# Identity matmuls in eight places ahead of TensorE's stages

## What is computed

```python
def first_block(x, ...):
    n1 = rmsnorm(h, norm1_g[l])
    proj = n1 @ w_in[l]                       # GLA and SGU branches, gates
    merged = sigmoid(ga) * (y_a @ w_branch_a) + sigmoid(gb) * (y_b @ w_branch_b)
    h = h + merged @ w_out[l]
    n2 = rmsnorm(h, norm2_g[l])
    h = h + peer(n2, ...)                     # 8 heads, top 16 of 128 x 128 experts each
    return rmsnorm(h, final_g)

def hybrid_layer(x, ...):
    x = x + 0.5 * rms_norm(swiglu(rms_norm(x, ffn1_pre_g), ...), ffn1_post_g)
    h = rms_norm(x, mix_pre_g)
    proj = h @ w_in                           # attention and SSM branches
    mixed = concatenate([attn, ssm]) @ w_out
    x = x + rms_norm(mixed, mix_post_g)
    x = x + 0.5 * rms_norm(swiglu(rms_norm(x, ffn2_pre_g), ...), ffn2_post_g)
    return x
```

## Time and profile before

| what | value |
|---|---|
| median of three runs | 1694.07 us |
| the profiled execution | 1692.44 us |
| its span, first to last instruction | 1690.7 us |
| PE busy | 1582.9 us (94%) |
| DVE busy | 1235.1 us (73%) |
| ACT busy | 795.9 us (47%) |
| POOL busy | 155.4 us (9%) |
| mean granted TensorE clock | 0.971 |
| matmul instructions in the records | 9080 |

### The profile page before, as it was taken

How to read it: one execution, slowest core, us unless ns; L and a number is a source line. 1 busy time by engine, 2 the same in 40 slices (tenths; PEclk the granted TensorE clock), 3 DMA queues, 4 the chain that set the end, 5 groups by cost and what they waited for, 6 DMA issues and landing times.

```text
span 1690.7 us, 25985 instructions
## 1 busy us (share of the span) xinstructions
PE 1582.9 (94%) x9080; PEld 1363.3 (81%) x9080; DVE 1235.1 (73%) x2038; ACT 795.9 (47%) x1212; POOL 155.4 (9%) x85
## 2 busy tenths in 40 slices
PE   6989889989999999999999999799997988879997
PEld 5777778879998888878888888688877967568886
DVE  4575559999998777677777777677777685367776
ACT  4544345447776343344444444544445653254443
POOL 1000257860000000000000000000001200000000
PEclk9999999999999999999999999899997989889999
DMA  5444334532324555555555555355552322345552
GB/s 199 175 147 171 131 125 163 187 125 100 115 108 151 197 198 189 183 174 199 180 192 191 183 196 198 137 191 189 183 194 78 139 75 100 125 139 196 185 187 99
DMA packets 38952, 270.40 MB, mean 160 GB/s; under 512 B 4705, under 2 KB 5217, under 8 KB 6642
## 3 DMA queue, kind: packets, MB, share of 16 engines
q1 hardware_dynamic: 37296, 266.97, 44.2%
q10 hardware_dynamic: 1602, 2.71, 0.5%
HBM read 268.62 MB, written 1.05 MB: 160 GB/s over the span
## 4 chain that ended last, share of the span: by engine, by line
PE 80%; DVE 15%; ACT 3%; issue 1%; DMA 1%; DVEq 0%; SPq 0%; ACTq 0%
PE ps L696 47%; PE ps L731 17%; PE ps L733 7%; PE ps L943 3%; DVE arena L1857 2%; PE ps L685 1%; DVE wlo L525 1%; PE ps L730 1%; DVE arena L1835 1%; PE ps L802 1%; DVE arena L1815 1%; DVE arena L1818 1%; DVE arena L1824 1%; DVE arena L1812 1%; DVE arena L1821 1%
## 5 line engine op out<-in xcount | busy, mean ns | idle before, releaser
L731 PE MATMUL ps<-XT,whi 128*128 128x512 f32 x1200 | 430.9, 399 | 1.9 <-DVE wlo L525 1.9
L696 PE MATMUL ps<-XT,whi 128*128 128x256 f32 x1696 | 315.6, 305 | 4.2 <-DVE wlo L525 4.2
L733 PE MATMUL ps<-XT,wlo 128*128 128x256 f32 x1050 | 295.6, 281 | 0.0
L504 ACT ACTIVATE whi<-raw 128x1024 fp32r<-128x1024 f32 x178 | 187.3, 1058 | 221.6 <-PE ps L696 161.2
L525 DVE TENSOR_TENSOR wlo<-raw,whi 128x1024 fp32r<-128x1024 f32 x146 | 186.5, 1289 | 121.5 <-ACT whi L504 120.2
L696 PE MATMUL ps<-whi,HAh 128*128 128x512 f32 x688 | 269.7, 392 | 5.5 <-DVE HAl L1943 3.0
L696 PEld LDWEIGHTS ps<-XT,whi 128*128 128x128 f32 x1696 | 268.0, 196 | 4.6 <-issue 4.6
L696 PE MATMUL ps<-wlo,HAh 128*128 128x512 f32 x688 | 268.8, 391 | 0.0
L696 PE MATMUL ps<-whi,HAl 128*128 128x512 f32 x688 | 268.3, 390 | 0.0
L731 PEld LDWEIGHTS ps<-XT,whi 128*128 128x128 f32 x1200 | 223.8, 189 | 47.4 <-DVE wlo L525 2.2
L733 PEld LDWEIGHTS ps<-XT,wlo 128*128 128x128 f32 x1050 | 199.6, 190 | 5.9
(11 more groups left out here) (267 smaller groups left out, 2104.1 us busy)
## 6 DMA issues: line engine op xcount, KB each, us to landing
raw<-in_experts SPq DMA_DIRECT2D x128, 1024.0 KB, 4.7
raw<-in_panels SPq DMA_DIRECT2D x58, 1024.0 KB, 4.8
raw<-in_ffa SPq DMA_DIRECT2D x33, 1024.0 KB, 4.8
raw<-in_ffb SPq DMA_DIRECT2D x33, 1024.0 KB, 4.8
arena<-in_row_post ACTq DMA_DIRECT2D x3, 512.0 KB, 3.7
X<-in_x SPq DMA_DIRECT2D x2, 512.0 KB, 5.3
out<-X SPq DMA_DIRECT2D x2, 512.0 KB, 2.7
arena<-in_row_ln ACTq DMA_DIRECT2D x2, 256.0 KB, 7.5
```

Of the source, the lines that this page charges most:

```text
L504: act.activation(whi[:, buf(p), :], half(item_of(p), p % 2), ACT.Copy).then_inc(part_hi, 1)
L696: last = pe.matmul(out, x if w_moving else w, w if w_moving else x, start=start and n == 0, stop=stop and n == 2)
L731: last = pe.matmul(out, wh[:, k], XT[:, k], start=k == 0, stop=k == NK - 1)
L733: pe.matmul(out[:, T:], wl[:, k], XTh[:, k], start=False, stop=False)
```

## The change

PE gets a helper `keep_turning`, which multiplies `ident` by `ident` n times into 128 columns of a bank, and `turn_ahead`, which first claims the second bank of the coming stage's transposes. It is called ahead of seven `transposes` calls, with n of 18, 30, 50, 62, 52, 36 and 50, and `keep_turning` alone with 20 ahead of the first `output`. That makes 318 matmuls. No other engine's list changes.

```diff
+            def keep_turning(out, n):
+
+                for _ in range(n):
+                    pe.matmul(out[:, 0:P], ident[:, :], ident[:, :], start=True, stop=True)
+
+            def turn_ahead(stage, n):
+
+                t_claim(pe, stage, 1)
+                keep_turning(t_bank(stage, 1), n)
...
+            turn_ahead("mg", 18)
             transposes("mg", tiles(XN, NK), waits=lambda j: (merged, 2 + j // 2 * 2))
...
+            turn_ahead("n2", 30)
             transposes("n2", tiles(XN, NK), norm=1)
...
+            turn_ahead("idx", 50)
             pe.wait_ge(sel_ready, 1)
             transposes("idx", [s[:, tt, :] for s in (I1S, I2S, GS) for tt in range(NT)])
...
             for i in range(4):
                 claim(pe, f"ex{i}")
+            keep_turning(bank("ex3"), 20)
             for n in range(UN):
                 output(n, S_PRE + n, S_PRE + n + 1, n % 2, start=(n == 0))
...
+            turn_ahead("ffa", 62)
             transposes("ffa", tiles(XN2, NK), norm=2)
...
+            turn_ahead("mix", 52)
             transposes("mix", tiles(XN2, NK), norm=3)
...
             pe.wait_ge(ssm_y, 1)
+            turn_ahead("ssm", 36)
             transposes("ssm", tiles(XS, NK))
...
+            turn_ahead("ffb", 50)
             transposes("ffb", tiles(XN2, NK), norm=4)
```

## The result

The changed kernel took 1712.62 us (median; 1708.64 to 1713.78), the kernel before 1694.28 us in the same measurement: ratio 1.0104, 95% interval 1.0091 to 1.0117. The medians are 18.3 us apart, and the ratio makes 17.6 us: the change is slower. The forecast was 1709.5 us. The profiled execution of the changed kernel is the 1708.64 us one, 16.2 us above the profiled execution of before.

The account below looks back on a forecast made before the run. PE was taken to carry 80% of the chain, mostly matmuls at full pace. Lateness of 28.9 us against 13.4 us given back made +15.5 us on the profiled 1692.44; the median forecast was 1709.5 us, range 1703 to 1721.

Parts of the forecast that it names:

- The price of an identity matmul: All 318 matmuls: 0.224 us each, bounds 0.112 and 0.244, holding PE for 71.2 us.
- rival 1: All identity matmuls: repeating the same weights costs no load, 0.112 us each, so faster, 1686 us; chance 0.12.
- The overshoot: Ahead of eight stages: identity matmuls outlast PE's waits by 1.5 to 8.1 us, 28.9 us of lateness together.
- What the clock gives back: In the stages: transposes and first matmuls at full instead of half clock return 13.4 us.
- The term of mg: Stage mg: 3.70 us from transposes to first matmul, overshoot counts as 0.5, clock returns 1.9; net -1.4 us.
- In idx the limit: Stage idx: gate products cannot follow PE fully because of ACT's factors; only 1.6 us comes back, net +2.2.
- The term of n2: Stage n2: 2.0 us overshoot, less 1.1 for transposes and 0.55 for matmuls at full clock; net +0.4 us.
- The sum: Whole kernel: net of all eight stages, 28.9 us of lateness against 13.4 given back, +15.5 us.
- Rival 2: Transposes lose the clock again; mg, n2, ffa, mix and ffb get nothing back, 10.2 us more, 1720 us; chance 0.08.
- 2 us either way: Estimated allowance for clock falls that stay, at two short waits in the mix and attention part, landing earlier or later.
- Rival 3: Identity matmuls do not hold the clock at all; 34.5 us on top of 28.9, 1757 us; chance 0.04.
- rival 4: Unread identity matmuls are dropped when the program is built; time stays at 1694 us; chance 0.03.

Follow-up runs that it names:

- after_again: The changed kernel run once more, unedited; median 1711.6 us, ratio 1.0096 to the kernel before.
- fit: Changed kernel with counts cut to the waits, ex's moved ahead of its waits, att served instead of ssm; 1687.01 us, ratio 0.9944.
- the fitted kernels: fit and fit_transpose, the kernels with counts cut to the waits and the gap behind the first transposes left open; 1687.01 and 1687.31 us.
- fit_half: Against fit, half of each count, so each wait begins with identity matmuls and ends idle; 1694.36 us, ratio 0.9999.
- fit_transpose: Against fit, each identity matmul replaced by transposes of the identity, with all counts doubled; 1687.31 us, ratio 0.9951.

## Why the prediction held, point by point

- **The price of an identity matmul.** 0.224 us was taken from other float32 matmuls; 0.223 was measured. Repeating the same operands costs no less, which rules out rival 1 (a faster kernel at 0.112 us).
- **The overshoot.** Foretold and measured, as the time from PE free to the first transposes: mg 4.03 and 4.02, n2 6.72 and 6.70, idx 11.20 and 11.17, ssm 8.1 and 8.04, ffb 11.20 and 11.16. `ex` began at the DVE result, 2.16 us into its idle time, as the order of the waits said.
- **What the clock gives back.** The 3.70 us from first transposes to first matmul, taken from ssm, came as 3.71 in ffa, mix and ffb. The term of mg was short by 0.4: its turn through ACT and DVE took 3.28 us, not 3.70. In idx the limit was where it was put: the gate products went 4.67 us after the first transposes (4.55 foretold), held by ACT's line 1357. The term of n2 was mis-sized: from its first matmul to the end of its matmuls PE gained 0.15 us (151.85 against 151.70) where 0.55 was counted. The missing 0.4 is a wait that the full clock brought out. PE did its first matmuls faster and then had to wait for DVE's copies (line 1698), so that this matmul came at 222.32 and not, at the pace of those before it, at 221.91. The prediction had put the limit only at the top-k work further on.

```profile
222.32 0.47 PE L706 MATMUL ps<-XT,whi 128*128 128x256 f32 x2 [0.16 <-DVE arena L1698]
```

- **The sum** came to 15.5 us against 16.2 in the profiled execution. Idx and ex, one row in the table, part at the point where PE is free ahead of ex (532.4 us before, 534.0 after): idx +2.5 where 2.2 was foretold, ex +2.1 where 2.0 was. A slip in it is small: ex is 3.5 - 0.46 x 3.4 = 1.9, not 2.0.
- **Rival 2 and the spread.** This is what the prediction had too small. Rival 2 was put as all or nothing, with 0.08, and 2 us either way were left for falls elsewhere. In the first profile none of the stages fell; in after_again n2 and ex did, and in fit mg, mix and ffb. A stage falls in one execution and not in the next, and the kernel before has such falls too, at a 2.1 us gap. The forecast took from one execution of ssm that the clock lasts through the gap between the transposes. For this change it did in 14 of 15 stages, in the fitted kernels of the same shape only in 3 of 10. One row could not tell these apart, so there is some luck in it. The medians' 18.3 us against 16.2 in the profiled pair is within this spread; what exactly it consists of in the executions that were not profiled is open.
- **Rival 3** (float32 matmuls of the identity do not hold the clock) and **rival 4** (they vanish) are answered by the rows at 1.00 and the 636 records.

## What to carry to other kernels

Filler matmuls in an in-order queue are paid in full as soon as they outlast the wait, so count them from their own issue spacing and the measured idle time, and put them ahead of the wait, not behind it. By the timelines above, this change paid some 30 us of lateness for some 14 us of clock. Half-filling the waits brought no time in fit_half, and in the fitted kernels the gap behind the first transposes had to be filled too to keep the clock. Look per stage, not at the mean clock: here it rose from 0.971 to 0.990 while the kernel became slower.

## What the runs showed of the hardware

- The same code at the same 2.1 us gap keeps its clock in one execution (window at 1.00, 19 records) and loses it in another (0.57, 12 records). The kernel before spread over 8 us, from 1690.6 us at a mean clock of 0.973 to 1698.9 at 0.968.
- A gap of 1.47 us between two groups of eight transposes can lose the clock too, after 8.2 us of dense matmuls (fit, mix).
- Dense transposes held a full clock for 9.3 us (fit_transpose).
- A matmul of an operand with itself, repeated, loads its weights every time: 636 loads for 636 records (both PE and PEld rose from 9080 to 9716).
